# First chunk's grams inside the attention, and one 128-row product in place of two in the chunk steps of a hybrid backbone

## The reference

```python
def step(s, inp):
    r_t, w_t, k_t, v_t, kk_t, a_t = inp
    sa = jnp.einsum("bhvk,bhk->bhv", s, -kk_t)
    s = (s * w_t[:, :, None, :] + sa[..., None] * (kk_t * a_t)[:, :, None, :]
         + v_t[..., None] * k_t[:, :, None, :])
    return s, jnp.einsum("bhvk,bhk->bhv", s, r_t)
```

## Time and profile before

| | |
|---|---|
| median of 3 runs | 2400.17 us (2395.78 to 2401.64) |
| the profiled execution | 2405.34 us, its span 2403.4 us |
| mean granted TensorE clock | 0.973 |
| busy in the span | PE 94%, PEld 71%, DVE 66%, ACT 53%, POOL 7% |
| chunk stages | 306.7 to 468.2 us (layer 0), 1146.1 to 1309.2 us (layer 1) |

### The profile page before, as it was taken

The page is one execution under the profiler, slowest core; times in us unless marked ns, Lnnn a source line. Parts: engine busy times, 40 slices in busy tenths (PEclk is TensorE's granted clock), DMA queues, the critical chain, the costliest instruction groups (busy, mean ns, idle before and its releaser), DMA issues.

```text
span 2403.4 us, 43271 instructions
## 1 busy us (share of the span) xinstructions
PE 2259.8 (94%) x17495; PEld 1713.5 (71%) x17495; DVE 1586.4 (66%) x1885; ACT 1262.4 (53%) x1522; POOL 164.9 (7%) x162
## 2 busy tenths in 40 slices
PE   5999888899999999999788899999999999999997
PEld 2445467746888885556677588888888888888886
DVE  3474556534333332675465489999989898989897
ACT  3341456413222223534464267777777777777775
POOL 0000045300000000000453000000000000000000
PEclk9999989999999999999799899999999999999998
DMA  7222610333232325220003679999999999999997
GB/s 295 70 88 70 241 51 17 114 148 123 88 105 88 101 88 221 71 90 35 11 17 112 255 280 351 357 360 355 358 359 364 341 368 348 369 349 368 343 371 261
DMA packets 237412, 504.63 MB, mean 210 GB/s; under 512 B 9958, under 2 KB 78844, under 8 KB 230236
## 3 DMA queue, kind: packets, MB, share of 16 engines
q1 hardware_dynamic: 235104, 488.44, 57.1%
q10 hardware_dynamic: 2172, 14.20, 1.5%
HBM read 492.12 MB, written 6.29 MB: 207 GB/s over the span
## 4 chain that ended last, share of the span: by engine, by line
PE 90%; DVE 3%; issue 2%; DMA 2%; ACT 1%; POOL 1%; ACTq 0%; SPq 0%; DVEq 0%; POOLq 0%
PE ps L615 18%; PE ps L616 18%; PE ps L617 18%; PE ps L705 11%; PE ps L608 7%; PE ps L919 7%; PE ps L643 2%; PE ps L954 1%; DVE tail L2136 1%; PE ps L1288 1%; PE ps L1075 1%; PE ps L1127 1%; DMA tail<-in_w_out 1%; PE ps L1254 1%; PE ps L1239 1%
## 5 line engine op out<-in xcount | busy, mean ns | idle before, releaser
L2440 DVE TENSOR_TENSOR weight_parts<-front,weight_parts 128x2048 fp32r<-128x2048 f32 x336 | 767.7, 2289 | 85.6 <-ACT weight_parts L1774 81.7
L1774 ACT ACTIVATE weight_parts<-front 128x2048 fp32r<-128x2048 f32 x336 | 643.5, 1919 | 248.1 <-PE ps L617 248.0
L615 PE MATMUL ps<-weight_parts,token_parts 128*128 128x512 f32 x1344 | 534.3, 398 | 1.7 <-issue 1.7
L616 PE MATMUL ps<-weight_parts,token_parts 128*128 128x512 f32 x1344 | 525.1, 391 | 0.0
L617 PE MATMUL ps<-weight_parts,token_parts 128*128 128x512 f32 x1344 | 524.8, 390 | 0.0
L615 PEld LDWEIGHTS ps<-weight_parts,token_parts 128*128 128x128 f32 x1344 | 253.2, 188 | 55.9 <-DVE weight_parts L2440 4.6
L617 PEld LDWEIGHTS ps<-weight_parts,token_parts 128*128 128x128 f32 x1344 | 252.9, 188 | 54.9
L705 PE MATMUL ps<-front,tail 128*128 128x512 f32 (+3 forms) x704 | 282.2, 557 | 6.5 <-ACT front L1455 4.4
L616 PEld LDWEIGHTS ps<-weight_parts,token_parts 128*128 128x128 f32 x1344 | 253.4, 189 | 48.9
L705 PEld LDWEIGHTS ps<-front,tail 128*128 128x128 f32 (+1 forms) x704 | 132.2, 190 | 147.3 <-issue 139.0
L919 PE MATMUL ps<-tail 64*64 64x64 f32 (+1 forms) x6976 | 170.5, 234 | 52.9 <-DVE tail L2136 21.2
(11 more groups left out here) (289 smaller groups left out, 2404.5 us busy)
## 6 DMA issues: line engine op xcount, KB each, us to landing
front<-in_exp_w SPq DMA_DIRECT2D x345, 1024.0 KB, 6.9
tail<-in_ffn_w SPq DMA_DIRECT2D x30, 1024.0 KB, 5.1
tail<-in_ada_w SPq DMA_DIRECT2D x27, 1024.0 KB, 8.6
tail<-in_w_in SPq DMA_DIRECT2D x24, 1024.0 KB, 5.1
front<-in_ada_w SPq DMA_DIRECT2D x21, 1024.0 KB, 11.5
tail<-in_w_out SPq DMA_DIRECT2D x8, 1024.0 KB, 8.1
parked_x<-front ACTq DMA_DIRECT2D x2, 2048.0 KB, 11.1
tail<-front SPq DMA_DIRECT2D x32, 128.0 KB, 2.3
```

Source lines behind the costliest of these rows:

```text
L615: mm(view, a_hi, b_hi, start=start, stop=False)
L616: mm(view, a_lo, b_hi, start=False, stop=False)
L1774: f_(whi[k % PARTS], at(A_RING2 + (k % RING2) * SLOT2, SLOT2), ACT.Copy).then_inc(cnt["act"].sem, 1)
L2440: ins = v.tensor_tensor(wlo[k % PARTS], at(A_RING2 + (k % RING2) * SLOT2, SLOT2), whi[k % PARTS], ALU.subtract)
```

## The change

1. The two grams of chunk 0, DVE's masks, ACT's removal copies and the turning of the values move from the head of `chunks` into the last units of `attention`. Banks 6 and 7, and later 0 to 3, are kept out of the rotation there, and `chunks` begins by waiting until the banks 0 to 3 are free. `attention_sums` moves behind level 3 of chunk 0, `attention_root` (ACT) and `modulation(2)` (DVE) to the end of step -1, `attention_inverse` (DVE) to the end of step 0. The tiles are laid out anew for this.
2. R becomes one product over 128 rows for n > 0. To this end SP copies the state's rows into the half of `VU` that later holds U (`s_rows`, four transfers a step, in pieces of 256 bytes), and the Z rows into the half of `GHT` that the removal copy has been taken from (`z_rows`, four transfers a step, two steps ahead). The product with Z from the state, which stood between level 1 and doubling 1, is gone.

```diff
 def attention(l):                                   # PE
                     if n < len(units):
                         scores(n)
+                    if n == len(units) - 1:
+                        banks.kept |= {P_OUT, P_OUT + 1}
+                        for b in (P_OUT, P_OUT + 1):
+                            pe.wait_ge(banks.free[b], banks.uses[b])
+                        pe.wait_ge(ev("rates_used"), 8 * (l + 1))
+                        gram(l, 0, 0)
+                        banks.turn = 0
+                    if n == len(units) + 1:
+                        gram(l, 0, 1)
+                        banks.kept |= set(range(P_SEQ))
+                        banks.turn = P_SEQ
...
                         turned(n - 2)
+                    if n == len(units) + 1:
+                        pe.wait_ge(ev("values_final"), CC * (l + 1))
+                        values_turned(l)
+                        banks.turn = P_SEQ
...
 def chunks(l):                                      # PE
-                for b in (P_OUT, P_OUT + 1):
+                banks.kept = set()
+                for b in range(P_SEQ):
                     pe.wait_ge(banks.free[b], banks.uses[b])
...
-                gram(0, 0)
-                values_turned()
-                gram(0, 1)
-                attention_sums(l)
-                for t in range(4):
-                    banks.released(pe, ("vr", l, t))
...
                         level(1, n + 1)
-                    if n > 0:
-                        pe.wait_ge(ev("s_ready"), (STEPS - 1) * l + n)
-                        small(("R", l, n), tokens(Za, n), of(S[m]), P_SEQ, straight, end=False
-                              ).then_inc(ev("straight"), 1)
...
                         pe.wait_ge(ev("v_rows"), 32 * (STEPS * l + n + 1))
                         if n > 0:
-                            after_straight(n, 0)
-                        small(("R", l, n), lambda d, cc, h: GHT[n % 3][d][halves[d], h, cc, 0, :],
-                              lambda d, cc, h: VU[d][halves[d], cc, h, :], P_SEQ, straight, begin=n == 0)
+                            pe.wait_ge(ev("z_rows"), 64 * ((STEPS - 1) * l + n))
+                            pe.wait_ge(ev("s_rows"), 64 * ((STEPS - 1) * l + n))
+                        rows_of = lambda d: slice(0, P) if n else halves[d]
+                        small(("R", l, n), lambda d, cc, h: GHT[n % 3][d][rows_of(d), h, cc, 0, :],
+                              lambda d, cc, h: VU[d][rows_of(d), cc, h, :], P_SEQ, straight)
...
                         level(3, n + 1)
+                    if n == -1:
+                        attention_sums(l)
 def attention(l):                                   # ACT
+                    if n == len(units):
+                        removal(l, 0, 0)
+                    elif n == len(units) + 1:
+                        removal(l, 0, 1)
 def chunks(l):                                      # ACT
-                removal(0, 0)
                 value_rows(0)
                 value_rows(1)
-                removal(0, 1)
                 begun(0)
-                attention_root()
...
+                    if n == -1:
+                        attention_root()
 def attention(l):                                   # DVE
                         weights(n - 1)
+                    if n >= len(units) - 1:
+                        for half in range(2):
+                            gram(l, 0, n - len(units) + 1, half)
 def chunks(l):                                      # SP
+                def z_rows(n):
+
+                    sp.wait_ge(ev("n0_ready"), 2 * (STEPS * l + n) + 2)
+                    for d in range(2):
+                        t_ = chunk_of(d, n) * CH
+                        for h in range(2):
+                            sp.dma_start(GHT[n % 3][d][halves[1 - d], h, :, 0, :], Za[d][halves[h], :, t_:t_ + CH]
+                                         ).then_inc(ev("z_rows"), 16)
+
+                def s_rows(n):
+
+                    sp.wait_ge(ev("s_ready"), (STEPS - 1) * l + n)
+                    for d in range(2):
+                        for h in range(2):
+                            sp.dma_start(VU[d][halves[1 - d], :, h, :], S[n % 2][halves[h], d]
+                                         ).then_inc(ev("s_rows"), 16)
...
                         sp.dma_start(VUs[halves[d], d], vrows[halves[c % 2], c // 2, :]).then_inc(ev("v_rows"), 16)
+                    if n:
+                        s_rows(n)
+                    else:
+                        z_rows(1)
+                    if n + 2 < STEPS:
+                        z_rows(n + 2)
```

More of the change, by code:

```diff
@@ L1011, in chunks @@
                     if pre:
-                        gram(n + 2, 0)
+                        gram(l, n + 2, 0)
                     if inv:
@@ L1563, in project, with removal @@
                         copy_out(("vg", l, cc), sigs[cc], lambda b: b, func=ACT.Sigmoid, bias=vcol("rwkv_v0", cc))
+            def removal(l, n, d):
+                banks.released(act, ("GH", l, n, d))
+                if d == 0 and (l, n) > (0, 0):
+                    act.wait_ge(ev("mt_ready"), mt_no(l, n, 0))
+                for h in range(2):
+                    ins = f_(N0[halves[(h + d) % 2], d], GHT[n % 3][d][halves[1 - d], h, :, 0, :], ACT.Copy)
+                ins.then_inc(ev("n0_ready"), 1)
             def attention(l):
@@ L1629, in keys_copied @@
                     copy_out(("KB", l, n), kb_of(l, n)[:, 1], lambda _: psum[P_OUT + 1])
-                def removal(n, d):
-                    banks.released(act, ("GH", l, n, d))
-                    if d == 0 and (l, n) > (0, 0):
-                        act.wait_ge(ev("mt_ready"), mt_no(l, n, 0))
-                    for h in range(2):
-                        ins = f_(N0[halves[(h + d) % 2], d], GHT[n % 3][d][halves[1 - d], h, :, 0, :], ACT.Copy)
-                    ins.then_inc(ev("n0_ready"), 1)
                 def exchanged(dst, src):
@@ L2074, in values, with gram @@
                                 ).then_inc(ev("values_final"), 1)
+            def gram(l, n, d, h):
+                banks.see(dve, ("GH", l, n, d))
+                bank = psum[P_OUT + h].rearrange("p (c a b) -> p c a b", c=CC, a=2)
+                to = GHT[n % 3][d][:, h]
+                if with_y(l, n):
+                    m = masks[:, d, 0:2, :].rearrange("p a b -> p (a b)").unsqueeze(1).broadcast_to([P, CC, P])
+                    ins = v.tensor_tensor(to.rearrange("p c a b -> p c (a b)"),
+                                          bank.rearrange("p c a b -> p c (a b)"), m, ALU.mult)
+                else:
+                    m = masks[:, d, 0:1, :].broadcast_to([P, CC, CH])
+                    ins = v.tensor_tensor(to[:, :, 0, :], bank[:, :, 0, :], m, ALU.mult)
+                if h:
+                    banks.done(ins, ("GH", l, n, d))
             def attention(l):
@@ L2239, in chunks @@
                         outputs(n)
+                    if n == -1 and l == 0:
+                        modulation(2)
+                    if n == 0:
+                        attention_inverse()
             def finish(l):
```

115 lines of the change are left out of this document (47 added, 68 removed).

## The result

The changed kernel takes 2410.11 us in the median of five runs (2409.16 to 2417.88), beside 2399.81 for the kernel before on the same chip: a ratio of 1.0059, 95% interval 1.0046 to 1.0072. That is 0.6% slower, 14.2 us by the ratio. The forecast was 2390 with a range of 2379 to 2402, so it is wrong, and in sign. The profiled execution took 2409.32 us.

What follows compares the result with a forecast made beforehand. PE's own sequence in the chunk stages was taken as the bound, code arrival nearly setting layer 0's steps. Terms -5.0, -7.5 and +2.4 gave -10.1 us, from a median of 2400.17 to 2390, range 2379 to 2402.

Steps and rivals of the forecast that it cites:

- late by 0 to 0.6: State rows in ordinary steps: the last lands 5.2 us after the output product, 0 to 0.6 late, 0.1 each.
- In layer 1 up to n = 4 the wait is for the state product, much earlier, and hidden.: State rows in layer 1's early steps: their copies wait only for the state product, so they cost nothing.
- rival (b): State rows late in every step, from issues of about 1.5 us each: 2411 us, slower; chance 0.12.
- Code arrival, -7.5: Steps n = 1 to 6: 32 fewer matmuls a step save code-block time, -4.8 in layer 0, -2.7 in layer 1.
- rival (a): Code arrival gives nothing back: blocks come later or chains set the step, 2399 us; chance 0.22.
- Part 1, -5.0: Grams and turned values moved into attention, sums into chunk 0: -0.5 us in layer 0, -4.5 in layer 1.
- The first level of layer 0: Start of layer 0's chunks: first level at about 311.6 in place of 317.38, 5.8 us earlier, ended by ACT.
- The sums inside chunk 0: Attention sums between level 3 and doubling 3 of layer 0: cost 3.9 us at full clock, 6.9 at half.
- Layer 1: First level near 1149.8 in place of 1156.28, -6.5 us; sums +1.2 to +2.4; net -4.5 taken.
- The last steps, +2.4: Step n = 7 of both layers: joint product waits for state rows, +1.5 us in layer 0, +0.9 in layer 1.
- the joint product's own greater length: R as one product over 128 rows: 1.12 us against 0.69, so 0.43 longer.
- The clock, rival (c): With less work PE is granted clock 0.5 for longer: +6 us, 2396; chance 0.14.

Runs made afterwards that it cites:

- part 1 alone: Kernel before with only item 1 of the change, R still two products with no copied rows: ratio 0.9969 to the kernel before, -7.4 us.
- part 1, no state product: Part 1 alone with the product of Z with the state left out, outputs not the reference's: ratio 0.9965 to the kernel before, -8.4 us.
- ACT copies: Changed kernel, but ACT copies the state's rows in place of SP's four transfers a step: ratio 0.9964 to the kernel before, -8.6 us.
- two queues: Changed kernel with two of the four state-row transfers issued by ACT in place of SP: ratio 1.0008 to the kernel before, +1.9 us.
- eight transfers: Changed kernel with the state's rows in eight half-size transfers a step in place of four: ratio 1.0253 to the kernel before, +60.7 us.
- no state rows: Changed kernel without copies of the state's rows, the joint product reading the step before's rows: one run, stages 132.6 and 137.4 us.
- ACT's copies with two products in the last step: Changed kernel with ACT copying the state's rows, and R as two products in each layer's last step: ratio 0.9964 to the kernel before.
- part 1 with the unused Z rows: Part 1 alone, plus SP's four Z-row transfers a step, which nothing reads: ratio 0.9959 to the kernel before, -9.8 us.

## Why the prediction was wrong

**The step that failed first: "late by 0 to 0.6", priced at 0.1 us a step.** PE's side of it was right: I had it ready 4.6 to 5.4 us after the last product that reads the tile, and it was ready after 4.4 to 5.2 (layer 0, n = 1 to 6). The landing was wrong. I had the last row at 5.2 us; the product began 5.9, 6.1, 6.6, 6.5, 6.5 and 6.5 us after. In the last steps of both layers, where each issue took 0.62 and the landing 2.3, it was 5.5, so the sum was nearly right for an undisturbed chain. But in five of those six steps one piece was slow: an issue of 1.56 to 1.68 (four steps), a landing of 2.9 in the fifth. Rows of before had both tails (1766 ns and 4.0 us); I took medians, for six transfers in a row. A chain of six rarely has six medians.

**"In layer 1 up to n = 4 the wait is for the state product, much earlier, and hidden."** Wrong too. The rows need `s_ready`, behind DVE's addition and POOL's decay, so the first state row was issued 3.4 to 4.2 us after that product and the last at 5.8 to 6.4; the joint product waited 0.9, 1.3 and 1.0 us in n = 1 to 3.

**The half of rival (b) that I priced wrongly.** It said that it decides from an issue of about 1.5 us each, and that at 1.0 it only eats the gain. It happened at a median of 0.617 and a mean of 0.73. Its time, 2411, was hit (2410.11), but by smaller waits and a fallen clock: that the two numbers agree is luck.

**Code arrival, -7.5.** This is where rival (a) was right, and it is the second half of the miss: -7.4 for part 1, -7.5 from the blocks and +22.8 for the waits would still have been slower, by 8 us and not by 14. Blocks of code do arrive as I read them: 107 packets became 104. Two things were wrong. I took 60.5 us of "issue" for PE's idle, where PE itself has 22.5 us in the whole kernel, about 11 of them in the stretch of each layer; this made code arrival look like the limit of every step. And I divided a step's matmuls by a rate. The records of the instruction queue, from the first level of chunk 1 to the end of n = 6 in layer 0, worked out from the trace:

```
kernel                     fetches   mean us from one to the next
before                     30        4.11
part 1 alone               30        4.10
part 1, no state product   28        4.20
ACT copies                 28        4.36
the change                 28        4.59
```

There are fewer, but they come further apart. In layer 0 of the kernel before 15 gaps of PE over 0.3 us were ended by "issue". In 14 of them PE went on 2.2 to 2.9 us after a fetch had begun, and the next fetch began 1.05 us later or more; the one at 445.63 us, 4.1 us after a fetch, doesn't fit. The shortest spacing is 3.4 us. My reading is that a block is not fetched far ahead here: one stretch of 126 matmuls costs the larger of some 3.4 to 4.0 us and its own chain, and what a stretch with DVE's waits takes beyond that is not made up by the next. Cutting 32 matmuls moves the block ends and leaves the waits; nearly nothing comes back. That this explains all of it is argued from these spacings, not shown by a run that changes the fetch. The Trainium skill, "Runtime: NRT & Kernel Launch", Instruction fetch mechanics, says that code comes in 16 KB blocks of 256 instructions over the sequencer's own queue, which fits 126 matmuls with their weight loads, and that crossing a block is mostly hidden. The first agrees; the second doesn't wholly here, where "issue" ended 22.5 us of PE's own idle before L919 in the kernel before.

**Part 1, -5.0.** Timed: -7.4 (-10.3 to -4.6). Its terms, from the changed kernel's trace:

- The first level of layer 0 was to come at 311.6, ended by ACT: it came at 305.76, ended by ACT. 5.7 of the 11.6 us came from the adaLN tile's bank, an edit whose place I had not looked up in the trace; without them it is at 311.4.
- The sums inside chunk 0 were to cost 3.9 to 6.9. From first level to first level of chunk 1 it is 23.19 in place of 18.92, so 4.3.
- Layer 1: last output of layer 0 to first level 682.95 in place of 688.04, -5.1 where I had -6.5, since POOL, not ACT, still ended the wait; the first inverse 24.19 in place of 20.54, +3.7 at half clock (+1.3 in part 1 alone).

**The last steps, +2.4.** They became 4.8 and 2.5 us longer. The start of the joint product was as forecast, 2.1 us later in layer 0 (I had 1.5) and 1.1 in layer 1 (0.9). The rest is the joint product's own greater length, which I had counted, and half clock behind that wait: it took 1.97 us, not 1.15. At full clock its price was right, 1.15 us where I had 1.12 (the last step of layer 0 with ACT's copies, at 456.41 us).

**The clock, rival (c).** I had it as a rival of its own, from less work. In layer 0 it grew with the waits: from 342 us to the last output none of before, part 1 alone and ACT's copies has a stretch at 1.2 GHz, two queues have 10.2 us of it, the change 20.5 (406.25 to 409.67 us, 440.38 to 450.62, 460.87 to 467.69), eight transfers 44.4. The waits aren't its only cause: three kernels without a wait for SP's state rows (no state rows, part 1 without the state product, ACT's copies with two products in the last step) have 3.4 us each, and part 1 with the unused Z rows has 6.8. In layer 1 every kernel has such stretches, 34 to 85 us of them from the first level on, and I can't say what sets their number; it stays open, and may be why the stages of single executions differ by several us where the timed ratios don't.

## What to carry to other kernels

Cost a chain of transfers by its length, and not by its medians: with six transfers in a row on one queue, 10 of the 14 chains here had a slow piece (an issue over 1.1 us, or 2.8 us or more from the last issue to the product), and the product waits for the last. If rows of this size must move inside a tight loop, let ACT copy them (four copies, 1.68 us, against 4.4 to 5.4 us from SP's first issue to the product in layer 0), and look beside whom the copying engine works.

Waits in a dense stretch of PE can cost more than themselves: eight transfers added 33.6 us of waits and 46.5 us of time, and the granted clock fell. Fewer instructions are not less time just because code arrives in blocks. And ask a view of idle time for PE alone, since a line of products counts the weight loads' idle too.

## What the runs showed of the hardware that I had not expected

- A DVE copy of 64x256 from one place in SBUF to another took 0.24 to 0.29 us with POOL idle and up to 1.27 us beside POOL, while DVE's additions from PSUM (128x512) took 0.69 us in both cases. 1.27 us is the length of one POOL product. The Trainium skill, "SBUF — State Buffer", SBUF: two separate sides, says that a DVE operation in a two-port mode and one of POOL share a pair of ports under an exclusive lock, held for a whole instruction. The lengths agree with such a lock; no row tells the mode of these copies. POOL itself, idle for some 7 us of a step, wasn't tried as the copier.
- An issue of a row transfer on SP took 0.6 us or 1.4 to 1.7 us, with one value of 0.98 between, in 56 of one kind.
- One PSUM bank given by rotation cost 5.7 us at a place far from the chunk stages: 3.67 us of waiting, and half clock about it (276.7 to 283.5).
